# Prompt attention of a decoder layer on TensorE: units of one key group's four heads, against units of two heads of both key groups with outputs summed in PSUM

## The reference

```python
# compressed blocks, selected blocks, sliding window; each with ALiBi
s = einsum('btgrd,bngd->btgrn', q, k) * (64 ** -0.5) - slope * dist
p = softmax(where(valid, s, NEG_INF))
o_branch = einsum('btgrn,bngd->btgrd', p, v)
o_nsa = g[:, :, 0] * o_cmp + g[:, :, 1] * o_slc + g[:, :, 2] * o_win
...
m = sigmoid(ga) * (o_nsa @ w_branch_a) + sigmoid(gb) * (o_hg @ w_branch_b)
out = m @ w_out            # then a top-4-of-32 mixture of experts
```

## Time and profile before

| what | us |
|---|---|
| median of 3 runs (lowest, highest) | 1576.51 (1572.67, 1577.09) |
| span of the profiled execution | 1575.1 |
| TensorE busy in it | 1447.4 |
| prompt phase, first scores to new_state(1) | 330.9 to 449.7 |
| end of the merge on TensorE | 524.1 |

### The profile page before, as it was taken

The page is one execution under the profiler, slowest core; times in us unless marked ns, Lnnn a source line. Parts: engine busy times, 40 slices in busy tenths (PEclk is TensorE's granted clock), DMA queues, the critical chain, the costliest instruction groups (busy, mean ns, idle before and its releaser), DMA issues.

```text
span 1575.1 us, 21206 instructions
## 1 busy us (share of the span) xinstructions
PE 1447.4 (92%) x8595; PEld 656.7 (42%) x8595; DVE 366.8 (23%) x845; ACT 297.0 (19%) x568; POOL 81.6 (5%) x108
## 2 busy tenths in 40 slices
PE   4999999979998969999999999999998998899896
PEld 4565455468876543333333333333332222232221
DVE  5210012346852451101010101011111100110123
ACT  4110004554530211111111111111110110011011
POOL 2000001200000000000000000000000000000000
PEclk9899999978999969999999999999999999999997
DMA  9690775413269579979999999999999999999994
GB/s 277 236 332 30 293 256 196 113 43 137 64 160 298 214 309 384 420 293 421 420 420 420 420 420 420 421 420 421 420 420 420 420 420 421 420 420 419 421 404 173
DMA packets 119927, 513.21 MB, mean 326 GB/s; under 512 B 12946, under 2 KB 42026, under 8 KB 68195
## 3 DMA queue, kind: packets, MB, share of 16 engines
q1 hardware_dynamic: 113090, 489.91, 78.8%
q0 software_dynamic: 6752, 22.06, 4.1%
HBM read 501.06 MB, written 19.22 MB: 330 GB/s over the span
## 4 chain that ended last, share of the span: by engine, by line
PE 61%; DMA 29%; DVE 5%; ACT 2%; SPq 1%; issue 1%; POOL 0%; DVEq 0%; POOLq 0%; ACTq 0%
DMA arena<-in_w_up 22%; PE bank L1335 20%; PE bank L1365 9%; PE bank L1177 4%; PE bank L785 4%; PE bank L1001 3%; PE bank L1002 3%; DMA arena<-in_w_in 2%; PE bank L1270 2%; DMA arena<-in_cache_cmp,arena 2%; PE bank L1327 1%; PE bank L1256 1%; PE bank L1258 1%; PE bank L1350 1%; PE bank L1075 1%
## 5 line engine op out<-in xcount | busy, mean ns | idle before, releaser
L1335 PE MATMUL bank<-arena 128*64 128x512 f32 x2176 | 493.7, 599 | 33.7 <-DMA arena<-in_w_up 33.7
L1335 PEld LDWEIGHTS bank<-arena 128*64 128x64 f32 x2176 | 145.1, 136 | 352.0 <-issue 266.9
L1365 PE MATMUL bank<-arena 128*64 128x512 f32 x1088 | 241.0, 595 | 0.0
L2247 DVE TENSOR_SCALAR arena<-bank,arena 128x1 uint32<-128x1 f32 x34 | 7.4, 219 | 592.3 <-PE bank L1343 592.3
L1365 PEld LDWEIGHTS bank<-arena 128*64 128x64 f32 x1088 | 75.0, 136 | 141.7 <-issue 135.8
L1710 ACT ACTIVATE arena<-arena 128x512 f32<-128x512 f32 x34 | 21.4, 630 | 528.8 <-DVE arena L2250 528.8
L1306 PE MATMUL bank<-arena 128*64 128x512 f32 (+1 forms) x420 | 103.5, 610 | 2.9 <-DVE arena L2208 2.9
L2321 POOL DMA_DIRECT2D slots<-arena x34 | 18.7, 551 | 1179.4 <-ACT arena L1717 1179.4
L1177 PE MATMUL bank<-arena 128*128 128x288 f32 x256 | 74.7, 442 | 2.3 <-DMA arena<-in_w_in 1.4
L2250 DVE TENSOR_SCALAR arena<-bank 128x512 f32<-128x512 f32 x34 | 23.5, 692 | 187.0 <-PE bank L1335 187.0
L1001 PE MATMUL bank<-arena 128*128 128x512 f32 (+1 forms) x112 | 57.0, 589 | 9.2 <-DMA arena<-in_w_in 6.5
(11 more groups left out here) (418 smaller groups left out, 1301.7 us busy)
## 6 DMA issues: line engine op xcount, KB each, us to landing
arena<-in_w_up SPq DMA_DIRECT2D x256, 1024.0 KB, 26.9
arena<-in_w_down SPq DMA_DIRECT2D x128, 1024.0 KB, 26.7
arena<-in_w_ada SPq DMA_DIRECT2D x12, 2048.0 KB, 11.7
arena<-in_w_in SPq DMA_DIRECT2D x6, 2048.0 KB, 13.2
arena<-in_w_in SPq DMA_DIRECT2D x16, 512.0 KB, 4.1
arena<-in_w_out SPq DMA_DIRECT2D x1, 4096.0 KB, 16.9
arena<-slots SPq DMA_DIRECT2D x2, 2048.0 KB, 10.2
out<-in_state_win SPq DMA_DIRECT2D x1, 4064.0 KB
```

What stands on the lines that cost most here:

```text
L1335: last = mm(banks[part][SLOT * s:SLOT * s + SLOT, :], xcT[:, q], ring[n % R_][:, D * part + 512 * s:D * part + 512 * s + 512], start=False ...
L1365: last = mm(banks[4][SLOT * s:SLOT * s + SLOT, :], lhs, ring[n % R_][:, D * v + 512 * s:D * v + 512 * s + 512], start=f == 0, stop=f == 7)
```

## The change

A unit is now `(i, branch, rp)`: query tile, branch and a pair of heads rp of **both** key groups. There are still 12 units of 4 heads, and they stand in the same place of the list.

- `scores`: same 4 products. Their order alternates between the key groups, whose keys and queries lie in SBUF rows 0 to 63 and 64 to 127; each group writes a bank of its own.
- `values`: the values (64 columns) are stationary and the transposed probabilities of two heads (256 columns) move. Per key tile 2 products instead of 4, one per group, written to PSUM partitions 0 to 63 and 64 to 127 of bank 3. All six units of a query tile add up in that bank, so `add` and the rows `on` are gone.
- The sum stands transposed already. `transposed_output` is gone; a ScalarE step `heads` copies the bank to `onT` once per query tile, and `values` of i = 1 wait for the first such copy.
- The scheduler's table has new costs for `scores` and `values`, so the order changes.

```diff
-UNITS = [(i, branch, g) for i in range(2) for branch in range(3) for g in range(G)]
+UNITS = [(i, branch, rp) for i in range(2) for branch in range(3) for rp in range(R // 2)]
...
-        step("pe", 1.0 + 0.5 * wide, "scores", (u,), ("biased", (u - 1,)))
+        step("pe", 0.7 + 0.45 * wide, "scores", (u,), ("biased", (u - 1,)))
...
-        step("pe", 0.5 * 4 * tiles, "values", (u,), ("probs_out", (u, tiles - 1)), ("add", (u - 1,)))
-        step("dve", 0.4, "add", (u,), ("values", (u,)), ("add", (u - 2,)))
+        step("pe", 1.0 * tiles, "values", (u,), ("probs_out", (u, tiles - 1)), ("values", (u - 1,)), ("heads", (i - 1,)))
+        if UNITS[u + 1:u + 2] == [] or UNITS[u + 1][0] != i:
+            step("act", 0.6, "heads", (i,), ("values", (u,)))
...
             def scores(u):
-                for r in range(R):
-                    key = kT[DH * g:DH * g + DH, branch - 1, 0:width] if branch else kcT[DH * g:DH * g + DH, NB * NCMP:NC_ALL]
-                    last = mm(banks[r // 2][:, 256 * (r % 2):256 * (r % 2) + width], qT[DH * g:DH * g + DH, r, P * i:P * i + P],
-                              key, start=True, stop=True)
+                for v in range(2):
+                    for g in range(G):
+                        key = kT[DH * g:DH * g + DH, branch - 1, 0:width] if branch else kcT[DH * g:DH * g + DH, NB * NCMP:NC_ALL]
+                        last = mm(banks[g][:, 256 * v:256 * v + width], qT[DH * g:DH * g + DH, 2 * rp + v, P * i:P * i + P],
+                                  key, start=True, stop=True)
...
             def values_of(u):
-                if u:
-                    pe.wait_ge(S("on"), u)
-                for r in range(R):
-                    for t in range(tiles):
+                if i:
+                    pe.wait_ge(S("onT"), i)
+                for t in range(tiles):
+                    for g in range(G):
...
-                        last = mm(banks[3][:, DH * r:DH * r + DH], pTp[u % 2][0:n, t, r], val, start=t == 0, stop=t == tiles - 1)
+                        last = mm(banks[3][DH * g:DH * g + DH, 256 * rp:256 * rp + 256], val, pTp[u % 2][0:n, t, 2 * g:2 * g + 2],
+                                  start=branch == 0 and rp == 0, stop=branch == 2 and rp == 1 and t == tiles - 1)
...
-            transposed_output()
+            pe.wait_ge(S("onT"), 2)
...
-            def output_T_out():
+            def heads_out(i):
+                act.wait_ge(S("p_pv"), len(UNITS) // 2 * (i + 1))
+                fn(onT[:, :, P * i:P * i + P], banks[3][:].rearrange("p (r t) -> p r t", r=R), ACT.Copy, scale=0.5
+                   ).then_inc(S("onT"), 1)
```

More of the change, by code:

```diff
@@ L174, in step @@
         todo[(name, args)] = (engine, us, before + same[-1:])
-    for u, (i, branch, g) in enumerate(UNITS):
+    for u, (i, branch, _) in enumerate(UNITS):
         wide = i + 1 if branch else 0.3
         tiles = max(1, int(wide))
-        step("pe", 1.0 + 0.5 * wide, "scores", (u,), ("biased", (u - 1,)))
+        step("pe", 0.7 + 0.45 * wide, "scores", (u,), ("biased", (u - 1,)))
         step("dve", 1.0 + 0.9 * wide, "biased", (u,), ("scores", (u,)), ("probs_T", (u - 2, UNITS[u - 2][0] if UNITS[u - 2][1] else 0)))
@@ L624, in load_gate @@
                              ).then_inc(S(f"ld_gp{j % 2}"), 16)
-            for j in range(len(INSIDE) + 2):
+            for j in range(min(NGATE, len(INSIDE) + 2)):
                 load_gate(j)
@@ L1100, in values_of @@
                             val = vcb[0:NCMP_P, NB, DH * g:DH * g + DH]
-                        last = mm(banks[3][:, DH * r:DH * r + DH], pTp[u % 2][0:n, t, r], val, start=t == 0, stop=t == tiles - 1)
+                        last = mm(banks[3][DH * g:DH * g + DH, 256 * rp:256 * rp + 256], val, pTp[u % 2][0:n, t, 2 * g:2 * g + 2],
+                                  start=branch == 0 and rp == 0, stop=branch == 2 and rp == 1 and t == tiles - 1)
                 last.then_inc(S("p_pv"), 1)
-            def transposed_output():
-                for i in range(2):
-                    if i:
-                        pe.wait_ge(S("onT"), 1)
-                    else:
-                        pe.wait_ge(S("on"), len(UNITS))
-                    for r in range(R):
-                        last = nc.tensor.transpose(banks[0][:, P * r:P * r + P], on[:, i, P * r:P * r + P], ident)
-                    last.then_inc(S("onT_ps"), 1)
             def hgrn_inputs(i):
@@ L1612, in gates_out @@
                 fn(gates[:, j], banks[7][:, 0:TP + NS], ACT.Tanh, scale=0.5).then_inc(S("gate_out"), 1)
-            steps = {"gates_out": gates_out, "exps": exps_of, "probs_out": probs_T_out, "inputs_out": hgrn_inputs_out, "decays": hgrn_decays,
+            steps = {"heads": heads_out, "gates_out": gates_out, "exps": exps_of, "probs_out": probs_T_out, "inputs_out": hgrn_inputs_out, "decays": hgrn_decays,
                      "end_decays": hgrn_end_decays, "keys_out": hgrn_keys_out, "result": hgrn_result_out,
@@ L1975, in biased_scores @@
                     dve.wait_ge(S("ppT_ps"), _tiles_before(u - 1))
-                for r in range(R):
-                    last = V.scalar_tensor_tensor(sP[u % 2][:, r, 0:width], nd, 2.0 ** -(R * g + r + 1),
-                                                  banks[r // 2][:, 256 * (r % 2):256 * (r % 2) + width], ALU.mult, ALU.add)
+                for g in range(G):
+                    for v in range(2):
+                        last = V.scalar_tensor_tensor(sP[u % 2][:, 2 * g + v, 0:width], nd, 2.0 ** -(R * g + 2 * rp + v + 1),
+                                                      banks[g][:, 256 * v:256 * v + width], ALU.mult, ALU.add)
                 last.then_inc(S("p_in"), 1)
@@ L1989, in probabilities @@
                 link(dve, "dve", V.reciprocal(pr_coef[:, four], pr_sum[:, four]))
-                at = 8 * branch + R * g
-                link(dve, "dve", V.tensor_tensor(pr_coef[:, four], pr_coef[:, four], sg_gate[:, i, at:at + R], ALU.mult))
+                coef = pr_coef[:, four].rearrange("p (g v) -> p g v", g=G)
+                gate = sg_gate[:, i, 8 * branch:8 * branch + 8].rearrange("p (g r) -> p g r", g=G)[:, :, 2 * rp:2 * rp + 2]
+                link(dve, "dve", V.tensor_tensor(coef, coef, gate, ALU.mult))
                 if branch == 0:
@@ L1996, in probabilities @@
                                 pr_coef[:, four].unsqueeze(2).broadcast_to([P, R, width]), ALU.mult).then_inc(S("p_probs"), 1)
-            def add_output(u):
-                i, branch, g = UNITS[u]
-                to = on[:, i].rearrange("p (r g d) -> p g r d", r=R, g=G)[:, g]
-                new = banks[3][:, 0:R * DH].rearrange("p (r d) -> p r d", r=R)
-                dve.wait_ge(S("p_pv"), u + 1)
-                if branch == 0:
-                    V.tensor_copy(to, new).then_inc(S("on"), 1)
-                else:
-                    dve.wait_ge(S("on"), u - 1)
-                    V.tensor_tensor(to, to, new, ALU.add).then_inc(S("on"), 1)
             after(dve, "gl")
@@ L2085, in hgrn_new_state @@
                     V.tensor_tensor(state, state, new, ALU.add).then_inc(S("state"), 1)
-            steps = {"biased": biased_scores, "probs": probabilities, "add": add_output, "distances": hgrn_distances,
+            steps = {"biased": biased_scores, "probs": probabilities, "distances": hgrn_distances,
                      "factors": hgrn_factors, "head_masked": hgrn_masked, "to_end": hgrn_to_end, "end_keys": hgrn_end_keys,
```

21 lines of the change are left out of this document (8 added, 13 removed).

## The result

The changed kernel took 1564.96 us (median of 20 runs, 1561.18 to 1571.73), the kernel before 1572.94 us in the same job (20 runs). The ratio is 0.9941, with a 95% interval of 0.9931 to 0.9952. By the ratio that is about 9.3 us, by the two medians 8.0, where I forecast 6.1. The profiled execution spans 1565.0 us, 10.1 less than before.

What follows compares the result with a forecast made beforehand. The prediction took TensorE to bound the prompt phase: 6.3 us saved on scores plus 4.3 on values minus 4.5 of new waits gave 6.1 off 1575.1, so 1569.0 us profiled and 1570.4 median, range 1565.5 to 1576.5.

Steps and rivals of the forecast that it cites:

- the new waits: TensorE waits at units 7 and 8, attention(1,0) and the recurrence's end: together 4.2 us, rounded up to 4.5 lost.
- the term of 6.3 us: Scores: row halves side by side cut 16.1 us to 9.8; saved 6.3 us, bounds 3.5 and 6.9.
- the term of 4.3 us: Values: column halves side by side, 256 columns moved, cut 14.4 us to 10.1; saved 4.3 us.
- my 1.5 at the end of the recurrence: Wait at keys_back, state and out, where the chain of VectorE and ScalarE does not shrink: about 1.5 us.
- one for one: Behind new_state(1), the state's store, block 12's load, merge and expert stream move with the phase's end.
- Booking the transposes at nothing: Phase end: dropping 8 transposes and two copies, covered by SyncE's 6.43 us issue, booked at nothing; uncovered some 2 us.
- The clock: Rival in the prompt phase: TensorE gaps bring three more slow places, +4.5 us, so 1575; chance 0.10.
- Weights one after the other: Rival in scores: row halves' weights load serially, saving 3.5; or waits double. 1574 us, chance 0.17 for both.
- Gain not passed on: Rival behind the phase: block 12's load ends by its own length after new_state(1); 1576.5 us, chance 0.05.
- The rule on weights for the values: Rival in values: 64 records pay their weights bare, 3.7 us back, 2.4 saved, 1574 us; chance 0.05.
- Denser steps that spare three slow gate halves: Rival in the prompt phase: denser TensorE steps spare three slow-clock places; 1566 us, chance 0.07.
- Slower: Rival in scores and values: neither kind of half overlaps in short steps; 5 us slower, 1581.5 us, chance 0.06.

Runs made afterwards that it cites:

- Kernel 5: Changed kernel with units of one key group again, values still stationary, 512 columns of probabilities moved, no adds or transposes: 1581.18 us, ratio 1.0054 to the kernel before.
- kernel 12: Kernel before with only the 8 transposes moved behind the samples' inputs and gate block 10: 1578.0 us, ratio 1.0014 to the kernel before.
- kernel 9: Changed kernel as it is, measured again in the last job: 1567.31 us (12 runs), ratio 0.9952 to the kernel before.
- kernel 10: Changed kernel with 8 transposes and 2 copies into an unread buffer put back at the phase's end: 1567.22 us, ratio 0.9952 to the kernel before.
- kernel 1: Changed kernel with a unit's score products ordered key group 0 twice, then group 1 twice: 1566.65 us, ratio 0.9926 to the kernel before.
- kernel 4: Changed kernel with the recurrence's attention products moving 64 columns (four copies of the 16): 1559.0 us, ratio 0.9884 to the kernel before.
- kernel 11: Changed kernel with the recurrence's attention products moving 64 columns instead of 16, repeated in the last job: 1558.26 us, ratio 0.9904 to the kernel before.
- kernel 8: Changed kernel with steps in the old order and the recurrence's attention products moving 64 columns: 1558.14 us, ratio 0.9899 to the kernel before.
- kernel 6: Kernel before with the recurrence's attention products moving 64 columns instead of 16: 1570.59 us, ratio 0.9974 to the kernel before.

## Why the prediction was right in kind and too small

**The mechanism** was right. Both kinds of halves run side by side in these short steps, and the phase, bound by TensorE, passed its gain on. Kernel 5, without pairs, is 0.54% slower than the kernel before. What failed is the size of three terms: the scores' and values' savings were priced too small (10.6 us together, 12.0 measured), and the new waits too large (4.5 us, 3.2 and 3.0 measured).

**Scores: the term of 6.3 us was a little too small.** Wide steps took 1.06 us for my 1.05, narrow ones 0.55 to 0.65 for my 0.7. With 0.62 that is 8 x 0.62 + 4 x 1.06 = 9.2 us, saved 6.9. The value lay at my own upper bound: I had the weights side by side at 0.62 and took 0.7 for caution. One of the eight narrow steps, unit 0's, gained nothing: it ends ahead of the phase's first inputs, which wait for VectorE until 334.7 us now and until 334.9 before. TensorE stands idle there for 3.39 us instead of 2.83.

**Values: the term of 4.3 us was too small.** They took 0.58 and 1.01 us for my 0.64 and 1.09: 8 x 0.58 + 4 x 1.01 + 0.6 = 9.3 us, saved 5.1. I had added a whole entry of 0.2 to records at 0.111; measured, one and two tiles differ by 0.43 for four records, so a record is 0.108 and the entry 0.15. Transposes behind two-tile values pay the same 0.15: 0.59 us at 407.77, and 0.44 at 410.75 behind a gate half. That with no entry the two sums would come out about 2 us better was a slip of mine: they hold 27 entries, 5.4 us at 0.2. The row L823 that I used for the bare price of weights does not alternate between halves, as I wrote; all its products write partitions 0 to 62. For a bare price that is the right kind of row.

The Trainium skill, "TensorE: Matmul & The Clock Gate", Part 3, says that weight loads overlap with running products only when the row group differs. By that the 64 weight columns of each record would be paid bare here; a step of 0.58 us for four records of 256 columns leaves no room for that beside kernel 5's 1.00 for two records of 512. The trace disagrees with the rule in this shape.

**The new waits: 4.5 us booked, 3.2 and 3.0 measured.** TensorE's idle time rose by 3.2 us (1.62 to 4.87), in a second pair of traces by 3.0 (1.80 in kernel 12, 4.75 in kernel 9). Units 7 and 8 held more than I said, 3.0 us for my 2.0. The 0.7 at attention(1,0) and the rounding of 0.3 did not come. Of my 1.5 at the end of the recurrence 0.38 stands ahead of `head` in the traces of both kernels, and 0.77 ahead of `keys_back` (L1147) is the rest. Changed kernel, and then kernel 12, where `keys_back` is L1154:

```profile
435.82 0.66 PE L1147 MATMUL bank<-arena 128*128 128x128 f32 x4 [0.77 <-DVE arena L2056]
```

```profile
443.72 0.66 PE L1154 MATMUL bank<-arena 128*128 128x128 f32 x4 [0.78 <-DVE arena L2075]
```

So this wait isn't new either. In the first trace of the kernel before it doesn't show, because the gate half ahead of it ran at the lower clock there (3.28 us at 441.71) and filled the time. I had added what the waits would be, without taking off what they were.

**The sum.** For the first pair of traces: 6.9 + 5.1 - 3.2 = 8.8 us, beside 9.0 measured as the earlier end of the phase. My sum had 6.1; the steps account for 1.4 of what is missing and the waits for 1.3. That this closes so well is in part luck, since it leaves out the clock, which differs from trace to trace. These are the phases from the first inputs to the end of new_state(1), kernel before:

```profile
334.88:449.74 114.86, 113.25 (x660) 95.33 (x660) 80.91 (x201) 56.42 (x162) 0.00 (x0) 0.91 0.26 81
```

Changed kernel:

```profile
334.71:440.79 106.08, 101.21 (x605) 76.41 (x605) 76.66 (x189) 57.18 (x163) 0.00 (x0) 0.92 0.28 89
```

Kernel 12, the kernel before but for its last steps:

```profile
333.19:448.67 115.48, 113.68 (x669) 96.12 (x669) 81.28 (x201) 56.27 (x161) 0.00 (x0) 0.91 0.26 81
```

Kernel 9, the changed kernel again:

```profile
330.80:439.41 108.61, 103.86 (x605) 78.15 (x605) 76.78 (x189) 57.18 (x163) 0.00 (x0) 0.89 0.28 87
```

The change shortens the phase by 8.8 us in the first pair and by 6.9 in the second. What the lower clock cost can be estimated as the length times what the column lacks to 1.00: 10.3 and 8.5 us in the first pair, 10.4 and 11.9 in the second, each to about half a microsecond. So the clock gave the change 1.8 us in one pair and took 1.6 in the other; without it the two pairs give 6.9 and 8.4.

**The end of the phase and one for one.** The 9.0 us were kept. Booking the transposes at nothing was right, kernel 10. The way from new_state(1) to the merge was 40.2 us before and 38.8 and 39.6 after. Where this comes from is open: SyncE's row for the store of the state is 6.43 us in the earlier trace rows and 5.45 after, and kernels 10 and 12 speak against gate block 10 and the transposes as its cause. Over all traces the row goes with the moment at which the phase ends: it is 5.35 to 5.75 us in the eight where new_state(1) was done by 444.3 us, and 5.98 to 7.21 in the six where it was done later. No run isolates what stands behind that.

**The clock** was a rival both ways. I had said that the prediction is wrong if the slow gate halves change in number, and they did: of more than 2.3 us there were five in the trace before (4.03, 2.38, 3.63, 3.47 and 3.28) and two in the first trace after (2.76 and 3.60). But the slow places partly moved to scores (2.01), values (1.12, 1.68 and 1.91) and an attention step (2.59), and the column over the phase hardly changed, 0.91 before, 0.92 and 0.89 after. That does not make the clock small: with 64 moved columns it is some 8 us behind the change, as much as the change.

**The absolute number.** The result's job put the changed kernel at 1564.96 us, half a microsecond below my range, beside a kernel before at 1572.94, 3.6 below the median I had built on. The last job put the same kernel at 1567.31 us beside 1575.46. The mean of the two ratios, 0.9947, is a gain of 8.4 us. The lesson is in the sum, 6.1 for some 8.4, and not in the half microsecond. My range allowed 11 us below the median I built on, and should have kept the scatter of its base, some 4 us, beside that of the change.

**My rivals.** Weights one after the other: refuted, narrow scores 0.65. The rule on weights for the values: refuted, 0.58. Gain not passed on: refuted. Denser steps that spare three slow gate halves: true of the first trace by their number, worth 1.8 us there and nothing in the second pair. Slower: refuted, but kernel 5 shows that it was one missing pair away.

## What to carry to other kernels

Where a step is a few short products, put both row halves or both column halves of the array into the same step: here such a step took 0.54 to 0.60 times as long as in one half. Take prices from rows with the same overlap and don't round caution into each term, since mine all leaned the same way and made half of the miss; and set a wait that you expect against the wait that already stands at that work. Compare two traces from the same piece of work on and not from the same microsecond. When a stretch has a clock column below 1.00, look at what stands ahead of it before changing anything else: here the edit of one step that moved 16 columns per product was worth some 8 us behind the rewrite, as much as the rewrite, and 4 us without it.

## What the runs showed of the hardware

- Products of different row halves overlap also where the program groups them by half: 0.65 and 1.07 us in kernel 1, beside 0.65 and 1.06 alternating.
- A step with 16 moved columns per product counts TensorE as busy from end to end (1.69 us in all of its 16 records) and yet goes with a lower clock behind it: in the changed kernel such a step at 417.04 is followed by one that took 2.59, values at 1.91 and a gate half at 3.60, while TensorE never stood idle between. Not every such step does this: those at 348.63, 356.99 and 365.15 were followed by gate halves of 2.06. With 64 moved columns the clock column was 1.00 from 340 to 440 us in kernel 4 and to the phase's end at 431.26 in kernel 11, also across 3.8 us of idle time in one stretch (in pieces of 1.3 us at most). It isn't the only cause: with 64 columns too one stretch was at 0.91 in the old order (kernel 8), behind 2.75 us of idle time in one piece, and two in the kernel before (kernel 6), where nothing was isolated.
- Two traces of the changed kernel differed by 0.8 us in the 39 us behind the phase, and by 2.5 us in the length of the phase (106.1 and 108.6 us), with 2.65 us of it in TensorE's busy time. Between traces of all kernels the start of the phase's inputs varied from 329.2 to 336.1 us. A term below a microsecond can't be read from one trace.
